# Expert stage of a two-layer MoE kernel: six prefetched experts in three pair groups by request, the other 26 ordered by a TensorE sort

## The reference, cut to what matters

```python
def hierarchical_moe(h, rg_w, rg_b, re_w, re_b, w_gate, w_up, w_down):
    ...
    expert_id = g_idx[..., None] * EXPERTS_PER_GROUP + top_i
    combine = jnp.sum(jax.nn.one_hot(expert_id, N_EXPERTS, dtype=jnp.float32) * top_w[..., None], axis=-2)
    hid = jax.nn.silu(jnp.einsum('bsd,edf->bsef', h, w_gate)) * jnp.einsum('bsd,edf->bsef', h, w_up)
    hid = hid * combine[..., None].astype(h.dtype)
    return jnp.einsum('bsef,efd->bsd', hid, w_down)
```

## Time and profile before

| | us |
|---|---|
| median of three runs | 1044.07 |
| lowest and highest | 1043.07, 1045.49 |
| the profiled execution, time | 1046.35 |
| its span | 1044.2 |
| PE busy | 873.0 (84%) |
| DVE busy | 304.0 (29%) |
| ACT busy | 177.0 (17%) |
| mean granted TensorE clock | 0.931 |

### The profile page before, as it was taken

How to read it: one execution, slowest core, us unless ns; L and a number is a source line. 1 busy time by engine, 2 the same in 40 slices (tenths; PEclk the granted TensorE clock), 3 DMA queues, 4 the chain that set the end, 5 groups by cost and what they waited for, 6 DMA issues and landing times.

```text
span 1044.2 us, 13222 instructions
## 1 busy us (share of the span) xinstructions
PE 873.0 (84%) x5572; PEld 583.7 (56%) x5572; DVE 304.0 (29%) x674; ACT 177.0 (17%) x387; POOL 26.5 (3%) x50
## 2 busy tenths in 40 slices
PE   4999999998986985679859998999998699567883
PEld 1787757876862442244338886587886345224321
DVE  2111323222557120101161233232346712110105
ACT  2101323210122110001021033142002211100001
POOL 0200000000000000000010000000000000000000
PEclk9899999999979998879979999999999889878997
DMA  9946963586648999999998315676555799999992
GB/s 378 409 181 276 384 242 125 205 286 249 280 189 327 432 426 430 430 412 396 426 422 348 148 34 198 274 293 242 161 242 192 292 430 429 428 428 428 427 426 106
DMA packets 38518, 324.48 MB, mean 311 GB/s; under 512 B 4920, under 2 KB 5048, under 8 KB 9392
## 3 DMA queue, kind: packets, MB, share of 16 engines
q1 hardware_dynamic: 34816, 313.02, 73.0%
q0 software_dynamic: 3200, 9.09, 2.7%
q10 hardware_dynamic: 432, 1.40, 0.3%
HBM read 321.06 MB, written 2.42 MB: 310 GB/s over the span
## 4 chain that ended last, share of the span: by engine, by line
PE 67%; DMA 21%; DVE 6%; issue 3%; ACT 3%; SPq 1%; DVEq 0%; ACTq 0%
DMA expert_gate_up<-in_w_gu 18%; PE ps L853 13%; PE ps L735 10%; PE ps L761 7%; PE ps L1014 6%; PE ps L928 5%; PE ps L1000 5%; PE ps L664 3%; PE ps L685 3%; DMA dense<-in_w_ada 2%; PE ps L875 2%; PE ps L965 2%; PE ps L823 2%; PE ps L705 2%; PE ps L886 2%
## 5 line engine op out<-in xcount | busy, mean ns | idle before, releaser
L853 PE MATMUL ps<-expert_gate_up,gathered_even 128*32 128x512 f32 x640 | 98.2, 679 | 57.6 <-DMA expert_gate_up<-in_w_gu 55.6
L735 PE MATMUL ps<-hT,dense 128*128 128x256 f32 x512 | 115.9, 385 | 0.0
L735 PEld LDWEIGHTS ps<-hT,dense 128*128 128x128 f32 x512 | 97.4, 193 | 16.1 <-issue 2.8
L853 PEld LDWEIGHTS ps<-expert_gate_up,gathered_even 128*32 128x32 f32 x640 | 28.9, 123 | 125.0 <-issue 125.0
L853 PE MATMUL ps<-expert_gate_up,gathered_odd 128*32 128x512 f32 x512 | 81.0, 592 | 7.1 <-DMA expert_gate_up<-in_w_gu 5.2
L761 PE MATMUL ps<-dense,hT 128*128 128x256 f32 (+1 forms) x320 | 69.4, 381 | 1.7 <-ACT hT L1130 1.7
L664 PE MATMUL ps<-dense,cond 128*32 128x256 f32 x768 | 55.3, 418 | 15.8 <-ACT cond L1223 11.8
L875 PE MATMUL ps<-expert_down,hiddenT 128*32 128x512 f32 x576 | 65.5, 594 | 2.3 <-ACT hiddenT L1194 2.3
L761 PEld LDWEIGHTS ps<-dense,hT 128*128 128x128 f32 x320 | 60.7, 201 | 10.4 <-ACT hT L1130 2.5
L1591 DVE TENSOR_TENSOR hidden<-hidden,ps 128x256 f32<-128x256 f32 x18 | 7.6, 421 | 200.8 <-ACT hidden L1190 200.8
L1014 PE MATMUL ps<-dense,zT 128*128 128x256 f32 x256 | 57.9, 388 | 4.2 <-DMA dense<-in_w_out 2.9
(11 more groups left out here) (239 smaller groups left out, 1029.2 us busy)
## 6 DMA issues: line engine op xcount, KB each, us to landing
expert_gate_up<-in_w_gu SPq DMA_DIRECT2D x64, 2048.0 KB, 18.2
expert_down<-in_w_dn SPq DMA_DIRECT2D x64, 1024.0 KB, 20.4
dense<-in_w_ada SPq DMA_DIRECT2D x48, 1024.0 KB, 9.1
dense<-in_w_in SPq DMA_DIRECT2D x28, 1024.0 KB, 11.8
dense<-in_w_o SPq DMA_DIRECT2D x8, 1024.0 KB, 6.1
dense<-in_w_out SPq DMA_DIRECT2D x8, 1024.0 KB, 4.8
dense<-in_w_c SPq DMA_DIRECT2D x4, 1024.0 KB, 28.4
dense<-in_w_uq SPq DMA_DIRECT2D x4, 576.0 KB, 6.0
```

The costliest lines, as they stand in the source:

```text
L735: last = mm(b[:, m * 256:(m + 1) * 256], w[:, k, m * P:(m + 1) * P], hT[:, k, :], start=(k == 0), stop=(k == KD - 1))
L853: last = mm(ps[32 * j:32 * j + 32, bank, :], xg[n % 2][:, k, at_ + j * CAP:at_ + (j + 1) * CAP], w_gu[BUFFER[held[j]]][:, k, :], start=(k ...
```

## The change

Six parts:

1. Experts 0 to 5, the prefetched ones, become groups 0 to 2, one pair of experts each, with tiles by request: for each expert one tile for the prompt's tokens and one for the latent ones. The other 26 are all sorted: the six fullest as pairs of tiles in groups 3 to 5, then 20 in five groups of four. There are 11 groups and `SPLIT` is 8. In `gate_up` only the last two groups go in halves.
2. `gather_first` takes the normalised tokens before scale and shift, as plain fp32 matmuls with 192 columns a request; scale and shift are applied in the copies (`gathered_first`) on ACT and DVE. The first gate/up no longer waits for the turned tokens, nor for their high and low parts; `turn_tokens` comes behind it.
3. Positions of experts 0 to 5 count from 1 within each request, so the selection of request 1 doesn't wait for the total of request 0. `normalise2` splits the second normalisation between ACT and DVE. `choose` is divided into `compare` and the rest, with `hidden2` of request 1 between.
4. The sort: PE makes the loads per partition (`totals`), DVE finds each expert's own rank on [64, 26] tiles, PE multiplies by the permutation to give order, positions and weights (`order_experts`, `turn_route`, `sort_route`).
5. The first three gate_ups run back to back, then the three turns, then their downs, scatters, and the first chunk's gather.
6. SP: down of expert 5 is loaded with its gate/up; experts 6 to 11 are all loaded after `order` (six gate/ups, then six downs); then group by group. `h2T` and `squares` move to other places in the arena.

```diff
-FIXED = 2 * EPI
+FIXED = SLOTS
-MAX_ROUNDS = 2 * P // CAP
-GROUPS = 9
-SPLIT = 5
-FIRST_OF = (0, 4, 8, 10, 12, 16, 20, 24, 28)
-PLACES_OF = ((0, 8), (8, 12), (12, 20), (20, 28), (28, 32))
+MAX_ROUNDS = 2 * P // (2 * CAP)
+GROUPS = 11
+SPLIT = 8
+TILES = ((0, 1, 0, 1), (2, 3, 2, 3), (4, 5, 4, 5), (6, 6, 7, 7), (8, 8, 9, 9), (10, 10, 11, 11), (12, 13, 14, 15),
+         (16, 17, 18, 19), (20, 21, 22, 23), (24, 25, 26, 27), (28, 29, 30, 31))
+BY_REQUEST = 3
+PLACES_OF = (((0, 6, 32),), ((6, 10, 64),), ((10, 12, 64), (12, 16, 32)), ((16, 24, 32),), ((24, 32, 32),))
...
                         gate_up_load(l, M[l], 5)
+                        down_load(l, M[l], 5)
                         first_gate_up(l, 3)
                         first_down(l, 3)
...
-                k, v = nth(l, ("tokens", 1))
-                sp.wait_ge(filled[k], v + 1)
-                down_load(l, M[l], 5)
-                for e in (6, 7):
-                    main_load(l, e)
-                for e in (6, 7):
-                    main_down(l, e)
                 sp.wait_ge(order_ready, l + 1)
-                for a in range(FIXED, FIRST_OF[SPLIT + 1], EPI):
-                    four_experts(l, a)
+                with ExitStack() as hold:
+                    which = [whose(hold, e) for e in range(6, 12)]
+                    for e in range(6, 12):
+                        main_load(l, e, which[e - 6])
+                    for e in range(6, 12):
+                        main_down(l, e, which[e - 6])
+                for g in range(6, SPLIT + 1):
+                    next_experts(l, TILES[g][0], TILES[g][-1] + 1)
...
             def gather_first(w, s):
 
                 for f in range(4):
+                    if s:
+                        pe.wait_ge(*reached(w, "xg_act", f + 1))
                     for k in (2 * f, 2 * f + 1):
+                        at_ = k % 2 * OWN
+                        last = mm(ps[:, FIRST_BANK[f], at_:at_ + OWN], xh2[:, s, k * P:(k + 1) * P],
+                                  sel[:, 0, s, 0:OWN].bitcast(F32), start=True, stop=True)
+                    last.then_inc(w["xg_filled"], 1)
...
+                turn_hidden2(l, 1)
+                router(l, 1)
+                count(l, 0)
                 ada(l, a0 + 2)
+                pe.wait_ge(*reached(m, "sel_ready", 1))
+                gather_first(m, 0)
+                ada(l, a0 + 3)
+                count(l, 1)
+                totals(l)
+                pe.wait_ge(*reached(m, "sel_ready", 2))
+                gather_first(m, 1)
+                order_experts(l)
+                gathered(m, 0)
...
+                gate_up(m, None, 0, 0)
+                turn_tokens(l, 0)
                 turn_tokens(l, 1)
+                gate_up(m, None, 1, 1)
+                gate_up(m, None, 2, 2)
+                for g in range(BY_REQUEST):
+                    turn_group(m, g, g, g)
+                pe.wait_ge(lo_ready, 4 * (l + 1))
+                pe.wait_ge(comb_ready, 2 * (l + 1))
+                select_T(m, 0, 3)
+                pe.wait_ge(*reached(m, "hidT_copied", 1))
+                select_T(m, 1, 0)
...
+                down(m, None, 0, 0)
+                turn_route(l)
...
+                scatter(m, 0, 0, True)
+                sort_route(l)
+                down(m, None, 1, 1)
+                pe.wait_ge(sorted_ready, l + 1)
+                select_T(m, 2, 0)
+                scatter(m, 1, 1, False)
...
+                gather(m, 1, (2, 3, 0, 2))
+                select_T(m, 3, 1)
+                gathered(m, 1)
+                down(m, None, 2, 2)
...
+            def normalise2(s):
+
+                V.tensor_scalar(xh2[:, s, 512:D], x[:, s, 512:D], mv[:, s, 0:1], rstd[:, 6 + s:7 + s], ALU.subtract,
+                                ALU.mult).then_inc(xh2_dve, 1)
...
+                normalise2(1)
+                compare(l, 0)
+                hidden2(l, 1)
                 choose(l, 0)
                 place(l, 0)
+                compare(l, 1)
                 choose(l, 1)
                 place(l, 1)
+                place_behind(l)
                 bias_ada(7 if l == 0 else 11)
                 sort_experts(l)
+                gathered_first(m, 1)
+                name_experts(l)
```

More of the change, by code:

```diff
@@ new lines, in turn_tokens, with totals, order_experts @@
+                    last.then_inc(tokens_filled, 1)
+            def totals(l):
+                pe.wait_ge(ada_biased, 8 if l == 0 else 12)
+                for h in range(2):
+                    for s in range(2):
+                        last = mm(ps[32 * h:32 * h + 32, ADA_BANK, 0:8], member[:, s, :], const[:, C_ONES:C_ONES + 8],
+                                  start=(s == 0), stop=(s == 1), skip_group_check=True)
+                last.then_inc(totals_filled, 1)
+            def order_experts(l):
+                pe.wait_ge(places_ready, l + 1)
+                mm(ps[0:1, ADA_BANK, 0:FREE], const[0:32, C_NAME:C_NAME + 1], perm[0:32, :], start=True, stop=True)
+                mm(ps[0:1, ADA_BANK, FREE:2 * FREE], own[0:32, 1:2], perm[0:32, :], start=True,
+                   stop=True).then_inc(order_filled, 1)
@@ new lines, in turn_route, with sort_route @@
+            def turn_route(l):
+                pe.wait_ge(comb_ready, 2 * l + 2)
+                for j, src in enumerate((pos, comb)):
+                    last = tr(ps[0:64, 1, j * P:(j + 1) * P], src[:, :, :].rearrange("p s e -> p (s e)"), ident)
+                last.then_inc(turned_filled, 1)
+            def sort_route(l):
+                pe.wait_ge(turned_ready, l + 1)
+                for j in range(2):
+                    for s in range(2):
+                        at_ = j * FREE
+                        last = mm(ps[:, s, at_:at_ + FREE], turned[32 * s:32 * s + 32, j, :],
+                                  perm[32 * s:32 * s + 32, :], start=True, stop=True)
+                last.then_inc(sorted_filled, 1)
@@ new lines, in place_behind @@
+            def place_behind(l):
+                b, gone = take(l, ("count", 1))
+                link(V.tensor_tensor(total[:, FIXED:NE], b[:, NE + FIXED:2 * NE], tot0[:, FIXED:NE], ALU.add))
+                V.tensor_copy(load[:, 0:FIXED], tot0[:, 0:FIXED])
+                V.tensor_copy(load[:, FIXED:2 * FIXED], b[:, NE:NE + FIXED])
+                link(V.tensor_tensor(ahead[:, FIXED:NE], b[:, FIXED:NE], tot0[:, FIXED:NE], ALU.add))
+                V.scalar_tensor_tensor(pos[:, 1, FIXED:NE], ahead[:, FIXED:NE], 1.0, member[:, 1, FIXED:NE], ALU.add,
+                                       ALU.mult).then_inc(gone, 1)
+                evacuated(l, ("count", 1))
@@ new lines, in name_experts, with turn_route @@
+            def name_experts(l):
+                dve.wait_ge(order_filled, l + 1)
+                V.tensor_copy(load[0:1, 2 * FIXED:2 * FIXED + FREE], ps[0:1, ADA_BANK, FREE:2 * FREE])
+                V.tensor_copy(order[0:1, :], ps[0:1, ADA_BANK, 0:FREE]).then_inc(order_ready, 1)
+                dve.wait_ge(order_ready, l + 1)
+            def turn_route(l):
+                dve.wait_ge(turned_filled, l + 1)
+                V.tensor_copy(turned[0:64, :, :], ps[0:64, 1, 0:2 * P].rearrange("p (j t) -> p j t", j=2)
+                              ).then_inc(turned_ready, 1)
@@ new lines, in sort_route @@
+            def sort_route(l):
+                dve.wait_ge(sorted_filled, l + 1)
+                for s in range(2):
+                    last = V.tensor_copy(by_load[:, :, s, :], ps[:, s, 0:2 * FREE].rearrange("p (j e) -> p j e", j=2))
+                last.then_inc(sorted_ready, 1)
+                dve.wait_ge(sorted_ready, l + 1)
+            def count_rounds(l):
+                n = 2 * FIXED + FREE
+                link(V.tensor_tensor(load[0:1, 0:n], load[0:1, 0:n], const[0:1, C_ROOM:C_ROOM + n], ALU.mult))
+                link(V.tensor_reduce(full[0:1, 0:1], load[0:1, 0:n], AX.X, ALU.max))
+                link(V.tensor_scalar(full[0:1, 1:MAX_ROUNDS], const[0:1, C_SLOT:C_SLOT + MAX_ROUNDS - 1], full[0:1, 0:1],
+                                     None, ALU.is_lt))
+                link(V.tensor_reduce(full[0:1, 8:9], full[0:1, 1:MAX_ROUNDS], AX.X, ALU.add))
+                V.tensor_copy(rounds[0:1, :], full[0:1, 8:9]).then_inc(rounds_ready, 1)
@@ L1602, in low @@
+                last.then_inc(w["selT_copied"], 1)
             def low(w, done, g):
@@ new lines, in _ @@
+                select_T(m, 0, 0, 3)
+                select_T(m, 1, 1, 0)
+                turn_route(l)
+                if l == 0:
+                    columns(7)
+                low(m, 0, 0)
+                sort_route(l)
+                select(m, 1, (0, 1))
+                low(m, 1, 1)
+                select_T(m, 2, 2, 0)
+                gathered(m, 1, (2, 3, 0, 2), 8)
+                select_T(m, 3, 3, 1)
+                low(m, 2, 2)
+                count_rounds(l)
+                for g in range(BY_REQUEST, GROUPS):
+                    n = chunk_of(g)
```

563 lines of the change are left out of this document (305 added, 258 removed).

## The result

| | us |
|---|---|
| changed kernel, median of four runs | 1063.01 |
| lowest and highest | 1058.26, 1063.79 |
| its profiled execution, and its span | 1058.26, 1056.3 |
| kernel before, median of four runs beside them | 1044.78 |
| ratio and its 95% interval | 1.0163 (1.0126 to 1.02) |

The change makes the kernel slower, by some 18 us. The prediction of 1057.0 has the right sign and is 6 us too low (0.7 of it is the kernel before, 1044.78 here and 1044.07 when the prediction was made); the range of 1043 to 1067 holds the result. The profiled execution is the fastest of the four, so its spans show some 5 us less than the median.

What follows compares the result with a forecast made beforehand. DMA was taken to bound the expert stages, TensorE elsewhere. Layer 0: -1.3 + 9.0 = +7.7; layer 1: -2.0 + 9.0 less some 2 recovered, +5.1; together +12.8 on 1044.07, so 1057 us, range 1043 to 1067.

Steps and rivals of the forecast that it cites:

- The stage as the start plus 7, plus 2.7, plus 182.8, plus idle: Expert stage: first gate/up's start, these terms in us, plus DMA idle for want of a free buffer.
- the 3 at the split: Layer 0's expert stage: 3 us more DMA time after TensorE's wait at the split, none in layer 1.
- The pair phase: First seven gate/ups of each expert stage: pairs run at TensorE's pace and starve DMA, 9.0 us a layer.
- The four holes: DMA idle between about 20 and 100 us after each first gate/up: 1.8, 1.9, 3.5 and 1.8 us.
- The sync engine's waits on gate/ups: Sign in the pair phase: SP should wait on gate/up of the pairs; no size given.
- The first gate/up of layer 1 recovered: Start of layer 1's expert stage: some 2 us formerly lost (8.98 against 7.11) taken as recovered.
- The front, a gain of 1.3 and 2.0 us: From last normalisation's end to first gate/up: N+20.5 in layer 0, N+16.3 in layer 1, gaining 1.3 and 2.0 us.
- A, pairs starve no one: Rival in the pair phase: the idle 9 us would vanish, giving 1039, or 1033 us; chance 0.12.
- B, a front at full clock: Rival ahead of the first gate/up: front at full clock, pairs still starve DMA, +7, 1051 us; chance 0.25.
- D, extra rounds: Rival in expert stages: extra rounds add a whole pass of 96 MiB, some 240 us; chance 0.01 or less.
- C, a cold clock in front and pairs: Rival in front and pair phase: half-rate gate/ups or front there give 1064 to 1071 us; chance 0.18.

Runs made afterwards that it cites:

- the second trace: The changed kernel itself, unaltered, run and traced again beside three edits of it: 1060.57 us, ratio 1.0153.
- the filled kernel: Five unread 128x512 matmuls added to the changed kernel in TensorE's idle wait ahead of the last normalisation's transposes: 1059.01 us, ratio 1.0149.
- two added edits: Idle wait filled with matmuls and sort moved behind the gathers, run together only with pairs spread too, against the changed kernel: 1041.90 us, ratio 0.9986.
- all three edits: Changed kernel with pair groups spread among fours, idle wait filled with matmuls, and sort moved behind the gathers: 1041.90 us, ratio 0.9986.

## Why the prediction was right in sign and 6 us low

**The stage as the start plus 7, plus 2.7, plus 182.8, plus idle: right.** The prediction read 412 to 432 GB/s in the slices of both stages; one slice of layer 0, at the split, stands at 396, where it took its 3 us in all the same. The sum gives E at S+204.5 in layer 0 (with the 3 at the split) and at S+201.5 in layer 1; measured 204.6 and 200.7, and 203.5 and 202.4 in the second trace.

**The pair phase: right.** The seventh gate/up was to end at S+100; it ends at S+100.6 and S+98.9. The four holes of 1.8, 1.9, 3.5 and 1.8 us, together 9.0, show as 3.3 (the first two in one window), 4.1 over the next two windows, and 1.3, together 8.7; in layer 1 they are 7.7. TensorE waits for gate/up weights from group 7 on only. Two runs show the cause and not only the fit: spreading the pairs gives back 9.5 us, and added work costs its full length there alone. The sync engine's waits on gate/ups, which the prediction named as a sign, are as long in the kernel before and show nothing.

**The first gate/up of layer 1 recovered: right.** Its rows of 3.64 and 3.64 (low and high part, overlapping) make 7.07 us instead of 8.98.

**The front, a gain of 1.3 and 2.0 us: wrong, and this is the step that failed.** From N, the end of the normalisation (0.95 ahead of T, where it was 1.31 before), the first gate/up was forecast at N+20.5 and N+16.3; it came at N+22.6 and N+21.6: a loss of 0.8 and 3.3 us. In place of -3.3 in the sum stands +4.1. (The terms of layer 0 also add up to N+19.5 at the end of the second gather, not N+19.) Two things were missed:
- A wait that the working did not have. `totals` stands in PE's order ahead of the second gather and needs the biased ada row, so PE idles 1.88 us in each layer with the gather queued behind it. Of these, 0.6 for positions were in the forecast, and 0.75 are left when `totals` stands behind the gather. The prediction let DVE's bias run beside TensorE and did not ask what PE had queued behind it.
- The clock in layer 1. The forecast kept the stretches of before, full from N+5.5 on. It was 0.50 over 800 to 811, and router, ada and first gather took 3.60, 1.94 and 3.98 us where 1.95, 1.07 and 2.87 are their full-rate values (the filled kernel's router, the other rows of these kinds at full rate): 3.6 us. Together with the 1.3 us of the wait that the forecast lacked, that is 4.9 of the 5.3 us missed. In layer 0 the wait and a second gather mostly at half rate (4.55, clock 0.66 over 311 to 316) outweighed a first that was faster than taken (3.40).

By S-E of both layers the stages cost 15.0 us in the first trace and 15.6 in the second (16.1 was forecast), the fronts 4.1: 19 to 20. The medians show 18.2 and 15.9, against a forecast of 12.8. So 7.4 us were missed in the front, and the final time is off by less because the stages came out up to 1 us cheaper and the rest of the kernel, of which the prediction says nothing, some 1 to 4: that part is luck. What lies between the stages differs by 4.4 us between two traces of the changed kernel (281.2 and 285.6 us from E to the next T; 284.5 in that of the kernel before), enough for what is left; no run says why.

**The rivals.** A, pairs starve no one, fell: the plain durations of TensorE's work already decide it. B, a front at full clock, did not happen by itself; it takes two added edits to get there, in layer 0. D, extra rounds, fell: gate/up has 1408 records, 64 for each of 11 groups in two layers, which is one round. C, a cold clock in front and pairs, came about by half: the front of layer 1, and a stretch in the pair phase of layer 0 of one trace (0.83 over 343 to 353, which costs 1.7 us). Its price in the front was underrated, since it was kept apart as a rival and not taken into the forecast. The Trainium skill, page TensorE: Matmul & The Clock Gate, section HAM oscillation, has TensorE fall back to the half rate in waits between bursts. For the wait of 4.38 us the traces agree: filled, transposes and router behind it run at full rate. For shorter ones they show both: behind 1.88 us the second gather took 4.55 in layer 0 and 2.87 in layer 1 of one execution, and behind 2.66 us the kernel before with its wait filled stayed at full rate in one run and fell to 0.50 in layer 0 of the other.

**The shorter chain is no shorter.** At its best the new order needs 14.8 and 16.4 us from T to S, with the wait filled and the sort moved; the old one needs 14.8 in both layers with the wait filled alone. The change took token turns and double gathers off this path, but in their place stands about as much: fp32 gathers of 2.87 us each, and a sort that PE takes part in.

## What to carry to other kernels

Before moving small groups together, compare bytes per group with engine time per group for each run of groups, not for the stage as a whole: the order alone was worth 9.5 us here, while a load among the larger groups cost nothing that could be told. Where a stage bound by DMA starts behind a thin chain of matmuls, look for the idle wait ahead of it first; four throw-away matmuls gave 4 to 5 us, and the restructured chain by itself lost 4. When an instruction is put into an in-order queue ahead of a critical one, its own wait joins the chain: ask for each what it waits for.

## What the runs showed that was not expected

A half-rate stretch avoided at one wait came back at the next: with the wait filled, the second gather took 4.55 us, and only with the sort moved too 2.87. That the two edits are therefore worth more together (9.2 us) than one by one (2.6 and 3.2) is likely, but the difference is within the noise. And the time of one kernel goes with its granted clock from run to run: among the twelve runs with all three edits the fastest, 1038.45 us, had a mean clock of 0.964 and the slowest, 1051.18 us, 0.951.
